# A mixture-of-experts kernel: the last three tiles' outputs kept on chip and combined by one-hot products, seven tiles of 128 rows in place of eight, gate/up refills in quarters for three buffers

## The reference

```python
p_group = softmax(t @ w_rg + b_rg)                 # 4 groups, the best one is taken
p_exp = softmax(logits of the 4 experts in it)     # the best two of them are taken
w_e = p of the two, scaled to sum 1, times the group's p
for each of 16 experts e:
    hid = silu(t @ w_gate[e]) * (t @ w_up[e])      # 1024 -> 512
    y += w_e * (hid @ w_down[e])                   # 512 -> 1024
x = x + g2 * y                                     # g2 depends on the condition c
out = rms_norm(x, final_norm)
```

## Time and profile before

| | |
|---|---|
| median of 3 runs | 782.32 us (781.32 to 784.16) |
| profiled execution: time | 781.9 us |
| profiled execution: span | 780.0 us |
| TensorE busy | 686.8 us, 88% |
| VectorE, ScalarE, GpSimd busy | 41%, 23%, 15% |
| mean granted clock of TensorE | 0.946 of full speed |
| bytes moved | 173.62 MB, mean 223 GB/s |
| chain of waits | TensorE 76%, VectorE 9%, GpSimd 4%, DMA 3% |

### The profile page before, as it was taken

How to read it: one execution, slowest core, us unless ns; L and a number is a source line. 1 busy time by engine, 2 the same in 40 slices (tenths; PEclk the granted TensorE clock), 3 DMA queues, 4 the chain that set the end, 5 groups by cost and what they waited for, 6 DMA issues and landing times.

```text
span 780.0 us, 9903 instructions
## 1 busy us (share of the span) xinstructions
PE 686.8 (88%) x3851; PEld 401.5 (51%) x3851; DVE 318.2 (41%) x752; ACT 180.0 (23%) x434; POOL 116.7 (15%) x164
## 2 busy tenths in 40 slices
PE   1799899999999999879999985899999999999830
PEld 1674446667666697545654455444444544443210
DVE  3203657856466533786612228350211211202126
ACT  3204215122121121456711141020111211201103
POOL 8700122313032155000000000010000000000030
PEclk9989999999999999899999986999999999999975
DMA  9999003793330300750085047638999999999965
GB/s 332 375 264 364 3 1 108 245 294 109 108 108 1 52 5 7 266 216 2 1 324 108 28 179 280 195 110 349 375 423 413 405 413 409 390 404 410 421 208 201
DMA packets 75475, 173.62 MB, mean 223 GB/s; under 512 B 21954, under 2 KB 38940, under 8 KB 71836
## 3 DMA queue, kind: packets, MB, share of 16 engines
q1 hardware_dynamic: 69520, 157.59, 56.0%
q0 software_dynamic: 2672, 9.44, 3.5%
q10 hardware_dynamic: 3228, 5.84, 2.0%
HBM read 156.59 MB, written 16.26 MB: 222 GB/s over the span
## 4 chain that ended last, share of the span: by engine, by line
PE 76%; DVE 9%; POOL 4%; issue 4%; ACT 3%; DMA 3%; POOLq 0%; ACTq 0%; DVEq 0%
PE ps L1031 14%; PE ps L1153 7%; PE ps L1064 7%; PE ps L2300 7%; PE ps L2267 5%; PE ps L1025 4%; PE ps L1059 2%; PE ps L2378 2%; PE ps L2264 2%; PE ps L2384 2%; DMA expert_rows<-yo 2%; PE ps L2291 2%; POOL lev L1648 2%; PE ps L653 2%; PE ps L2388 2%
## 5 line engine op out<-in xcount | busy, mean ns | idle before, releaser
L1031 PE MATMUL ps<-gu,xgT 128*128 128x512 f32 x256 | 113.0, 600 | 3.6 <-DVE xgT L1110 2.5
L1031 PEld LDWEIGHTS ps<-gu,xgT 128*128 128x128 f32 x256 | 48.6, 192 | 63.2 <-issue 63.2
L2300 PE MATMUL ps<-hT,winr 128*128 128x512 f32 x144 | 72.6, 612 | 0.0
L1540 POOL DMA_INDIRECT xg<-xn_rows,list x15 | 13.9, 928 | 384.7 <-DVE list L1447 185.9
L1153 PE MATMUL ps<-wout,yT 128*128 128x512 f32 x128 | 57.6, 610 | 0.0
L1064 PE MATMUL ps<-dn,hidT 128*128 128x512 f32 x128 | 56.5, 594 | 0.0
L1753 POOL TENSOR_TENSOR cc<-low,lev 128x512 f32<-128x512 f32 x20 | 30.2, 1518 | 129.5 <-DVE low L2087 104.0
L1891 DVE SCALAR_TENSOR_TENSOR acc<-ada,st,acc 128x512 f32<-128x512 f32 x56 | 48.5, 866 | 1.3
L2267 PE MATMUL ps<-hT,wind 128*128 128x512 f32 x96 | 43.4, 605 | 0.0
L1025 PE MATMUL ps<-gu,xgT 128*32 128x256 f32 (+1 forms) x384 | 43.0, 452 | 0.0
L1153 PEld LDWEIGHTS ps<-wout,yT 128*128 128x128 f32 x128 | 24.6, 195 | 30.0 <-issue 30.0
(11 more groups left out here) (433 smaller groups left out, 1046.6 us busy)
## 6 DMA issues: line engine op xcount, KB each, us to landing
dn<-in_w_down SPq DMA_DIRECT2D x16, 2048.0 KB, 23.3
gu<-in_w_gate SPq DMA_DIRECT2D x15, 2048.0 KB, 21.5
gu<-in_w_up SPq DMA_DIRECT2D x15, 2048.0 KB, 26.0
ada<-in_w_ada SPq DMA_DIRECT2D x12, 2048.0 KB, 11.6
expert_rows<-zero SPq DMA_DIRECT2D x12, 512.0 KB, 6.7
expert_rows<-yo ACTq DMA_DIRECT2D x8, 512.0 KB
wout<-in_w_out SPq DMA_DIRECT2D x1, 3072.0 KB, 10.6
x<-in_x SPq DMA_DIRECT2D x2, 1024.0 KB, 6.2
```

The source lines that it names most:

```text
L1031: ins = nc.tensor.matmul(PS[2 * b + w][:, :], T["xgT"][:, k, :], w_in[:, w, k, :], start=(k == 0), stop=(k == KT - 1))
L2300: ins = t.matmul(bank[:, :], w(k), T["hT"][:, k, :], start=(k == 0), stop=(k == KT - 1))
```

## The change

*Sizes.* `[128] * 7 + [64] * 5 + [32] * 4`, and 13 extra tiles in place of 12. `ORDER` is now 0, 1, 2, 12, 3, 11, 4, 10, 5, 9, 6, 8, 7, 13, 14, 15, in rows: 128, 128, 128, 32, 128, 64, 128, 64, 128, 64, 128, 64, 64, 32, 32, 32.

*Refills.* Gate/up of places 3, 4 and 5 come in quarters, each behind a quarter of the products of tiles 0, 1, 2.

*Outputs.* Tiles 13, 14 and 15 are not stored. `dve_output` writes each into 32 partitions of `yc` (96 rows used, the first 32 set to zero). VectorE builds for each token a one-hot row times its weight (`in_row`), TensorE transposes it (`pe_onehot`), ScalarE copies it to `back`. At the end `pe_back` adds up on TensorE, for each 128 tokens, the second rows times their weights (a diagonal matrix `diag` by `y2`) and the on-chip rows (`back` by `yc`); VectorE adds the sum to `x2`. The weights of first and second rows are zero where the row is on chip. The swap now puts rows of place 12 second.

*Gathers.* `y1` is gathered when place 11 is stored and the gate/up products of place 13 are done, `y2` when place 12 is stored. VectorE adds `w1 * y1` in the iteration of place 14. All branches for extra tiles come behind one branch on whether there are any.

```diff
-SIZES = [128] * 8 + [64] * 4 + [32] * 4
+SIZES = [128] * 7 + [64] * 5 + [32] * 4
+CHIP = 3
...
 def sync_moe(sp):
-                if n == NBUF:
+                if n < 2 * NBUF:
+                    b = n - NBUF
                     for part in range(4):
                         if part < 3:
-                            sp.wait_ge(sem("first_gu_mm"), part + 1)
+                            sp.wait_ge(sem("first_gu_mm"), 3 * b + part + 1)
                         else:
-                            sp.wait_ge(sem("gu_mm"), 1)
+                            sp.wait_ge(sem("gu_mm"), b + 1)
...
+    def pe_onehot(pe):
+        pe.wait_ge(sem("routing"), ROUTING["onehots"])
+        pe.wait_ge(sem("yo_d"), ONEHOT_AT + 1)
+        for i in range(ST):
+            ins = nc.tensor.transpose(PS[5][:, i * P:(i + 1) * P], T["in_row"][:, 0, i, :], idf[:])
+        ins.then_inc(sem("routing_pe"), 1)
+
+    def pe_back(pe):
+        pe.wait_ge(sem("routing"), ROUTING["route_i"])
+        pe.wait_ge(sem("exp_out"), 3)
+        for i in range(ST):
+            pe.wait_ge(sem(f"y_in{i}"), 16)
+            if i == 2:
+                pe.wait_ge(sem("yo_d"), E + 1)
+            for w in range(2):
+                nc.tensor.matmul(PS[2 * i + w][:, :], T["diag"][:, i, :], T["y2"][:, i, w * 512:(w + 1) * 512],
+                                 start=True, stop=False)
+            pe.wait_ge(sem("yo_d"), E + 1)
+            for w in range(2):
+                ins = nc.tensor.matmul(PS[2 * i + w][:, :], T["back"][:, i * P:(i + 1) * P],
+                                       T["yc"][:, w * 512:(w + 1) * 512], start=False, stop=True)
+            ins.then_inc(sem("oproj_mm"), 1)
...
 def dve_output(dve, n):
         dve.wait_ge(sem("dn_mm"), n + 1)
+        if on_chip(n):
+            dve.wait_ge(sem("yo_d"), E - CHIP + 1)
+            dve.wait_ge(sem("xg_tr"), E)
+            if n == E - 1:
+                nc.vector.memset(T["yc"][0:32, :], 0.0)
+            to = slice(32 * (n - E + CHIP + 1), 32 * (n - E + CHIP + 2))
+            for w in range(4):
+                rows, c = slice(32 * w, 32 * w + 32), slice(256 * w, 256 * w + 256)
+                ins = nc.vector.tensor_tensor(T["yc"][to, c], PS[4][rows, 0:256], T["g2q"][rows, :], ALU.mult)
+            ins.then_inc(sem("yo_d"), 1)
+            return
...
 def dve_moe(dve):   # after w1, w2
+        link(v.tensor_scalar(virtual, slotf, 32.0 - CHIP_ROW, None, ALU.add))
+        for n, w in enumerate((w1, w2)):
+            for i in range(ST):
+                ins = v.tensor_scalar(T["in_row"][:, n, i, :], T["row_n"][:], virtual[:, n, i:i + 1], w[:, i:i + 1],
+                                      ALU.is_equal, ALU.mult)
+        link(ins)
+        v.tensor_tensor(T["in_row"][:, 0], T["in_row"][:, 0], T["in_row"][:, 1], ALU.add).then_inc(sem("routing"), 1)
...
+            if n == E - 2:
+                dve.wait_ge(sem("y1_in"), 16 * ST)
+                for i in range(ST):
+                    x = T["x2"][:, i, :]
+                    ins = v.scalar_tensor_tensor(x, T["y1"][:, i, :], w1[:, i:i + 1], x, ALU.mult, ALU.add)
+                link(ins)
         dve_output(dve, E - 1)
+        for i in range(ST):
+            dve.wait_ge(sem("oproj_mm"), ST + i + 1)
+            for w in range(2):
+                x = T["x2"][:, i, w * 512:(w + 1) * 512]
+                ins = v.tensor_tensor(x, PS[2 * i + w][:, :], x, ALU.add)
+            ins.then_inc(sem("x3"), 1)
...
 def pool_moe(pool):
-        pool.wait_ge(sem("yo_st"), 16 * STORED[E - 1])
+        pool.wait_ge(sem("gu_mm"), E - CHIP + 1)
+        pool.wait_ge(sem("yo_st"), 16 * STORED[E - CHIP - 1])
         for i in range(ST):
             rows_back(0, "y1_in", i)
...
-        pool.wait_ge(sem("yo_st"), 16 * STORED[E])
+        pool.wait_ge(sem("yo_st"), 16 * STORED[E - CHIP])
         for i in range(ST):
             rows_back(1, f"y_in{i}", i)
```

163 lines of the change are left out of this document (108 added, 55 removed).

## The result

The changed kernel takes 785.38 us in the median of 20 runs (777.26 to 789.45), the kernel before 777.54 in 20 runs (773.32 to 784.16; the 782.32 of the first three was high). The ratio is 1.0076, 95% interval 1.0053 to 1.0098: slower by 0.76%, 5.9 us. It goes by the means of the fast runs, that is without the one of 789.45; the medians would give 1.0101. The forecast was no change, sum -0.1.

What follows compares the result with a forecast made beforehand. The prediction took DMA and TensorE as bounds side by side, TensorE 1.9 us behind at the end. Last down product +5.4, tail -5.5 and start +0.4 were summed to -0.1: 781.8 us, 782 on the median's scale, range 777 to 787.

Steps and rivals of the forecast that it cites:

- sum -0.1: Whole kernel: all forecast terms together change the span by -0.1 us, to 779.9.
- Sizes, -2.5: Expert loop: fewer rows gathered (-1.1) and stored (-1.4) bring the last down weights 2.5 us earlier.
- Quarter refills, -3.0: Expert loop: earlier gate/up loads of places 4 and 5 bring later weights 3.0 us earlier, bounds 0 to -4.7.
- VectorE ahead of the loop, +0.4: Before the first tile: two more chained operations for the tile's start row and their waits cost 0.4 us.
- Gathers among the weights, +12.1: End of the loop: output gathers take 12.1 us of DMA time from the last weights, bounds 0 and +13.
- Last product, +1.9 for the clock: Place 15: after TensorE's wait, gate and up products start at a low clock, 3.66 + 1.9 us.
- +5.4: End of the last down product: 753.3 us against 747.95, so 5.4 us later.
- The tail, -5.5: Last down product to final norms: 16.2 us in place of 21.7, saving 5.5 us.
- A: Last weights: they keep their pace despite the gathers; 769.6 us, or 775.7 with half the cost; chance 0.24.
- B: Tail: its 14 products may run at 1.2 instead of 2.4 GHz, up to 12.0 us more; chance 0.14.
- C: Place 14: VectorE's first-row additions hold up the last down product if gathers land after 745, up to 787; chance 0.07.
- D: Tile sizes: an expert overflows its smaller tile, adding over 40 us; chance 0.03 together with others.

Runs made afterwards that it cites:

- e5: The kernel before with the sizes 7, 5, 4 alone; ratio to the kernel before 0.9999.
- r1: The kernel before, unchanged, profiled a second time; span 772.0 us.
- e1: The kernel before with the new sizes and the quarter refills, outputs stored and gathered as before; ratio to the kernel before 0.9988.
- e8: The changed kernel with all eight output gathers issued once the last down weights have landed, first rows added one by one; ratio to the kernel before 0.9988.
- e3: The changed kernel without the four gathers of the first rows, so its output is not the reference's; ratio to the kernel before 1.0033.
- e6: The kernel before with the quarter refills alone; ratio to the kernel before 1.0025.
- e4: The changed kernel with the additions of the first rows moved behind the output of the last tile; ratio to the kernel before 1.0088.
- e7: The changed kernel with the old sizes 8, 4, 4 and whole refills, leaving the outputs on chip alone; ratio to the kernel before 1.0106.
- e9: e8 with the gathers issued earlier, when gate and up weights of the last tile have landed; ratio to the kernel before 1.0066.
- e12: e9 with 40 useless products on TensorE ahead of the last gate and up products; ratio to the kernel before 1.0073.
- e10: e9 with whole refills of buffers 1 and 2; ratio to the kernel before 1.0078.
- e14: e9 with only the second rows' four gathers issued at that point, the first rows' four waiting for the last down weights; ratio to the kernel before 1.0055.
- e17: e8 with one gather issued when the last gate and up weights land and the memset ahead of the last down products; ratio to the kernel before 1.0030.
- e11: The changed kernel with 40 useless products on TensorE ahead of the last gate and up products; ratio to the kernel before 1.0090.
- e13: e9 with the gathers replaced by eight plain reads of the same size from consecutive rows, issued by ScalarE; ratio to the kernel before 0.9966.
- e15: e13 with the plain reads issued by GpSimd in place of ScalarE; ratio to the kernel before 0.9943.
- e16: e9 with each of the first four gathers waiting for the one before to land; 785.54 us in a single execution.
- e18: e17 with paced gathers: two issued when the last gate and up weights land, each later one when the one two before has landed; ratio to the kernel before 0.9961.

## Why the prediction was wrong

The mechanism was there, place by place: a DMA full to its last load, TensorE waiting some 10 us for place 15, gathers among the weights, additions covered, a full clock in the long products. What failed is the sum, in two of its steps: the end of the last down product, and the saving in the tail. Term by term:

1. *Sizes, -2.5:* measured -0.1 (e5, +254.5 for +254.6; its ratio of 0.9999, 0.9974 to 1.0024, leaves room for 2 us). In the 250 us from the first product the weights' queue moved 80.60 MB before, 80.54 in r1 and 80.63 in e5; what fewer rows freed did not become weights. A share of 1.02 says that the engines are occupied, not that each byte less is time won. A part was not there to be had: places 4 to 13 store 896 rows before and not the 960 of the prediction, which take in place 14, whose store is issued at 741.84; that is 0.7 of the 1.4 us.
2. *Quarter refills, -3.0:* measured -1.5 (e5 to e1). The issues are not late: 516.24 and 538.16 stand 23.7 and 45.6 us behind the first product, where the forecast of 513 and 535 has 23.4 and 45.4. But 2.9 MB of weights gained by +60 had shrunk to 1.1 MB at +88 and 0.6 MB at +100, as the queue ran dry while the next loads waited for TensorE. The prediction took off 1.3 us for this; it cost more.
3. *VectorE ahead of the loop, +0.4:* nothing that shows; the loop starts at 489.7 us in the mean with the old routing and at 489.5 with the new.
4. *Gathers among the weights, +12.1:* +9.5 (e8 to after); a gather set costs +4.7 (e3 to after) or +4.8. Bandwidth was rightly taken as the cause: the weights land that much later. The price was set too high: in 722:756 the 4.19 MB of gathers hold 30.7% of the engines, 10.4 us or 2.5 us a MB, where the sum had 2.9.
5. *Last product, +1.9 for the clock:* the gate and up products took 5.07 us, and were hidden behind the weights; the down products took 3.50 in place of 1.93 (clock 0.66 in 755:760), which the sum did not have: +1.6. It takes the place of the 1.9 us by which TensorE was behind the weights before.

Sum to the end of the last down product: -0.1 - 1.5 + 9.5 = +7.9 for the weights, which the profiles show as +8.0 (+262.6 for +254.6); the product follows them by 3.6 us, before by 3.8. So it ends 7.9 us later, where **+5.4** was forecast. This is the first step that failed: the gains set against the gathers were 5.5 us in the sum and 1.6 measured, which the cheaper gathers made good only in part (weights +6.6 forecast, +8.0 measured); and the last down product ran at the low clock.

6. *The tail, -5.5:* the new one is 16.6 us (758.81 to 775.39; forecast 16.2). The old one was taken as 21.7, from the single execution that I had. In r1, e5, e6 and e1, which have the same tail, it is 19.2, 19.1, 19.9 and 20.2. So the saving is about 3. This is the second step that failed. Of the 2.4 us between the first profile and r1, 1.6 are VectorE's late start behind the last product (2.1 us for 0.5), the hold by gathers in a row.

7.9 - 3 = 4.9 us, against the 5.9 (4.1 to 7.6) measured; the remaining 1 us lies within that interval and is not put down to anything.

The rivals: A fell; the weights paid for every gather. B fell for the long products (clock 1.00 in 760:775) and held for the last down product (3.50 us for 1.93, 0.66 in 755:760), which it had not named. C was real and hidden in the changed kernel (e4), and cost 5.2 us in e7, where the weights came earlier. D did not occur. None of them was the hold of the other engines by gathers in a row, which in the changed kernel itself lies under its wait for weights: from 725 to 728 TensorE shows gaps of 0.3 to 0.5 us (issue) behind the gathers of 722.17, SiLU is late until 728.25, and then TensorE waits for place 15 all the same. It counted as soon as that wait was taken away (e9), and explains why the obvious repair, gathers beside the last 2 MB alone, gave back only 0.1%.

## What to carry to other kernels

A transfer moved out of a tail into a stretch in which the DMA is full costs about its own bandwidth there, while bytes saved there may come back as nothing, and loads issued earlier may only move the hole; so measure the gains by themselves (e5, e1) before setting them against a cost. Take the length of a stretch that is to vanish from more than one execution: 2.5 of the 5.5 us expected of the tail were in a single profile alone, and most of them stood in its rows as a late start with no local reason ("remote"). Where other engines have work to do beside them, row-list gathers are safer issued with pauses, at most two in flight, than in a row; here most of the gain over the changed kernel came already from moving them behind the weights (e8).

## What the runs showed of the hardware

- Seven or eight row-list gathers issued in a row by GpSimd (one each 1.24 us) held up TensorE (e12), TensorE or ScalarE (e9, e10, e14) or VectorE (e17) for 5 to 7 us, until 0.3 to 2.3 us behind the last of them. Four in a row did so for 2 to 4.5 us in the kernel before, e6, e7, e11 and the changed kernel, and not in r1, e5 and e4. The same bytes by plain reads (e13, e15) and gathers in ones or twos (e16, e18) did not. In e8, with eight in a row from 741.89 on, nothing was held up. Why it strikes one engine or execution and not another is open. The chip is not the reason by itself: e9 (hold) and e18 (none) ran on the same one, and so did e14 and e13. One candidate is the supply of instructions: the Trainium skill (Runtime: NRT & Kernel Launch, section on instruction fetch mechanics) says that each engine's sequencer fetches its pages through a DMA queue of its own. The records of the instruction queues show none between 734 and 753 in e9, but one at 747 and one at 748 in e17, inside its hold, so they do not settle it.
- Where the DMA is full for the later part of the loop, 0.5 MB less of input gathers and stores (96 and 32 rows of 4 KB, e5) brought no more weights: 80.63 MB in the 250 us from the first product, against 80.60 and 80.54 in the kernel before.
- The start of the loop wandered over 8 us between profiled executions (484.3 to 492.6). The two of the kernel before differ by 5.3 us there and by 3.0 us in all that follows up to the norms.
